# Last row tiles of a decoder step: stores from another queue, and sums ahead of the last turns

## The reference

```
x = x + (silu(ua_c) * ub) @ ffn_down              # 2816 -> 1024 features
y = x * rsqrt(mean(x * x, axis=-1) + 1e-6) * norm_final
y_prompt, y_sample = y[16:1040], y[1040:1072]     # stored as rows, one per token
```

## Time and profile before

| | |
|---|---|
| three runs | 1876.35, 1876.5, 1870.95 us; median 1876.35 |
| the profiled execution | 1874.11 us, of it 1872.3 us span |
| TensorE busy | 1722.2 us (92% of the span), mean granted clock 0.956 |
| VectorE, ScalarE, POOL busy | 1268.0 (68%), 682.0 (36%), 350.2 us (19%) |
| last `down` matmul ends | about 1849.0 us |

### The profile page before, as it was taken

The page is one execution under the profiler, slowest core; times in us unless marked ns, Lnnn a source line. Parts: engine busy times, 40 slices in busy tenths (PEclk is TensorE's granted clock), DMA queues, the critical chain, the costliest instruction groups (busy, mean ns, idle before and its releaser), DMA issues.

```text
span 1872.3 us, 30833 instructions
## 1 busy us (share of the span) xinstructions
PE 1722.2 (92%) x12025; PEld 1623.0 (87%) x12025; DVE 1268.0 (68%) x2319; ACT 682.0 (36%) x1207; POOL 350.2 (19%) x236
## 2 busy tenths in 40 slices
PE   4959999899999869988779989999999999999995
PEld 4834999899999857776679988999999999999995
DVE  4373766788888968867444378777777776575553
ACT  3253011121211146665542155333333334564442
POOL 0544143222222331132236220000000000000000
PEclk7979999999999979999889999999999999999997
DMA  7133211122222021343646212222222213866452
GB/s 261 46 92 93 57 46 40 54 67 92 85 80 63 15 102 64 119 146 132 208 129 245 93 47 80 81 82 80 70 81 87 75 58 117 292 200 210 153 181 77
DMA packets 161878, 201.28 MB, mean 108 GB/s; under 512 B 20057, under 2 KB 123449, under 8 KB 161201
## 3 DMA queue, kind: packets, MB, share of 16 engines
q1 hardware_dynamic: 142516, 124.66, 22.2%
q0 software_dynamic: 14256, 55.27, 8.9%
q10 hardware_dynamic: 4978, 19.59, 2.8%
HBM read 163.27 MB, written 35.61 MB: 106 GB/s over the span
## 4 chain that ended last, share of the span: by engine, by line
PE 53%; DVE 4%; ACT 3%; issue 2%; DMA 1%; POOL 0%; DVEq 0%; ACTq 0%
PE ps L2303 23%; PE ps L2696 13%; PE ps L229 6%; PE ps L1894 3%; PE ps L1938 2%; PE ps L1876 1%; PE ps L1860 1%; PE ps L1949 1%; PE ps L1975 1%; DMA down_raw<-in_ffn_down 1%; ACT probs L2082 0%; PE ps L2688 0%; DVE probs_turned L2160 0%; DVE operand_lo L3157 0%; DVE up_P_lo L3119 0%
## 5 line engine op out<-in xcount | busy, mean ns | idle before, releaser
L229 PE MATMUL ps<-act_hi,w_hi 128*128 128x358 f32 (+1 forms) x1080 | 360.8, 334 | 12.1 <-POOL act_lo L464 5.5
L2303 PE MATMUL ps<-operand_hi,up_P_hi 128*128 128x268 f32 x1232 | 354.3, 288 | 8.9 <-issue 6.7
L229 PE MATMUL ps<-act_lo,w_hi 128*128 128x358 f32 (+1 forms) x1080 | 354.9, 329 | 0.0
L229 PE MATMUL ps<-act_hi,w_lo 128*128 128x358 f32 (+1 forms) x1080 | 354.0, 328 | 0.0
L2303 PE MATMUL ps<-operand_lo,up_P_hi 128*128 128x268 f32 x1232 | 353.4, 287 | 0.0
L2303 PE MATMUL ps<-operand_hi,up_P_lo 128*128 128x268 f32 x1232 | 353.0, 287 | 0.0
L2303 PEld LDWEIGHTS ps<-operand_hi,up_P_hi 128*128 128x128 f32 x1232 | 233.9, 190 | 9.4 <-issue 7.0
L2303 PEld LDWEIGHTS ps<-operand_lo,up_P_hi 128*128 128x128 f32 x1232 | 233.4, 189 | 0.0
L2303 PEld LDWEIGHTS ps<-operand_hi,up_P_lo 128*128 128x128 f32 x1232 | 233.4, 189 | 0.0
L229 PEld LDWEIGHTS ps<-act_hi,w_hi 128*128 128x128 f32 (+1 forms) x1080 | 204.5, 189 | 14.5 <-issue 11.8
L229 PEld LDWEIGHTS ps<-act_lo,w_hi 128*128 128x128 f32 (+1 forms) x1080 | 205.0, 190 | 1.2
(11 more groups left out here) (423 smaller groups left out, 3128.0 us busy)
## 6 DMA issues: line engine op xcount, KB each, us to landing
down_raw<-in_ffn_down SPq DMA_DIRECT2D x132, 256.0 KB, 3.0
w_raw<-in_w_in SPq DMA_DIRECT2D x32, 512.0 KB, 3.9
w_raw<-in_ffn_up SPq DMA_DIRECT2D x48, 256.0 KB, 3.4
inner_save<-xt SPq DMA_DIRECT2D x22, 536.0 KB, 2.7
xt<-in_ffn_up SPq DMA_DIRECT2D x40, 256.0 KB, 3.4
inner_raw<-inner_save SPq DMA_DIRECT2D x44, 192.0 KB, 3.8
x_save<-xt SPq DMA_DIRECT2D x1, 4296.0 KB, 12.8
mix_b<-row ACTq DMA_DIRECT2D x8, 537.0 KB, 3.6
```

The costliest lines, as they stand in the source:

```text
L229: last = pe.matmul(core.acc(out_set)[0:rows, c, :], w(k), b(k)[:, c * CH:(c + 1) * CH], start=(i == 0 and n == 0), stop=(i == kblocks - 1 ...
L2303: last = pe.matmul(out[:, c, :], w[:, 128 * k:128 * k + 128], b(k)[:, cols], start=(name in OPENING and k == 0 and n == 0), stop=(k == 3 a ...
```

## The change

Five things, all in the stage above:

1. SP stores row tiles 6, 7 and 8 and the sample rows (new `store_row` in SP's block, semaphore `last_stored`), and waits for the four at its end. POOL stores row tiles 0 to 5 and waits for those.
2. In the last pass VectorE adds a square to the total after each eviction but the first (`between`); the last one follows.
3. TensorE turns features 0 to 6 of tiles 6 and 7, then of tile 8, then sums over features, and then turns feature 7 of the three tiles.
4. The copy of the sums out of PSUM is dropped: VectorE scales straight from PSUM, for the last third in two instructions.
5. The semaphore `y_taken` goes; in the first two thirds TensorE waits for the first count of `y_own` instead, before it turns the second row tile over the sums.

```diff
@@ block.sync
+        def store_row(t):
+            sp.wait_ge(out_a, t + 1)
+            sp.wait_ge(out_d, t + 1)
+            sp.dma_start(core.o["y_prompt"][0][128 * t - META:128 * t + QROWS[t] - META], rows[t % 3][0:QROWS[t], :])\
+                .then_inc(last_stored, 16)
+
+        for t in (6, 7, 8):
+            store_row(t)
+        sp.dma_start(core.o["y_sample"].rearrange("b s d -> (b s) d"), rows[(NT - 1) % 3][QROWS[-1]:ROWS[-1], :])\
+            .then_inc(last_stored, 16)
+        sp.wait_ge(last_stored, 64)
@@ block.tensor
+        def turn(t, k):
+            return pe.transpose(ysrc(t)[:, 128 * k:128 * k + 128], x[:, k, 128 * t:128 * t + ROWS[t]], core.c["ident"])
+
         def turn_rows(t):
-            n = ROWS[t]
             for k in range(KB):
-                if t == 6:
-                    pe.wait_ge(y_gain, 2 * KB + k + 1)
-                last = pe.transpose(ysrc(t)[:, 128 * k:128 * k + 128], x[:, k, 128 * t:128 * t + n], core.c["ident"])
+                last = turn(t, k)
             last.then_inc(turned, 1)
...
                 elif y == 1:
-                    pe.wait_ge(y_taken, third + 1)
+                    pe.wait_ge(y_own, ROOT_LINKS * third + 1)
...
-        turn_rows(6)
-        turn_rows(7)
+        for k in range(KB - 1):
+            pe.wait_ge(y_gain, 2 * KB + k + 1)
+            for t in (6, 7):
+                turn(t, k)
+        for k in range(KB - 1):
+            turn(8, k)
         sum_y(2)
-        turn_rows(8)
+        pe.wait_ge(y_gain, 3 * KB)
+        for t in (6, 7, 8):
+            turn(t, KB - 1).then_inc(turned, 1)
@@ block.gpsimd
-        for third in range(3):
-            if third < 2:
-                for s in (2 * third + 2, 2 * third + 3):
-                    pool.wait_ge(x_back[s % 2], 16 * (s // 2))
-                    x_reload(s)
+        for third in range(2):
+            for s in (2 * third + 2, 2 * third + 3):
+                pool.wait_ge(x_back[s % 2], 16 * (s // 2))
+                x_reload(s)
             for t in range(3 * third, 3 * third + 3):
                 store_row(t)
-        pool.dma_start(core.o["y_sample"].rearrange("b s d -> (b s) d"), rows[(NT - 1) % 3][QROWS[-1]:ROWS[-1], :])\
-            .then_inc(stored[(NT - 1) % 3], 16)
         for z in range(3):
-            pool.wait_ge(stored[z], 16 * (4 if z == 2 else 3))
+            pool.wait_ge(stored[z], 32)
         pool.wait_ge(states_stored, 32)
@@ block.vector
-        def evict(s):
+        def evict(s, between=None):
...
+                if between and m:
+                    between(m - 1)
...
             if third < 2:
-                dve.tensor_copy(ss, core.flat(7, 16)[:, cols]).then_inc(y_taken, 1)
+                dve.tensor_scalar(mean, core.flat(7, 16)[:, cols], 1.0 / D, EPS, ALU.mult, ALU.add).then_inc(y_own, 1)
             else:
-                dve.tensor_copy(core.ss[:, 6:8], core.flat(7, 16)[:, 6:8])
-                dve.tensor_copy(core.ss[0:ROWS[-1], 8:9], core.flat(7, 16, ROWS[-1])[:, 8:9]).then_inc(y_taken, 1)
-            dve.wait_ge(y_taken, third + 1)
-            dve.tensor_scalar(mean, ss, 1.0 / D, EPS, ALU.mult, ALU.add).then_inc(y_own, 1)
+                dve.tensor_scalar(core.mean[:, 6:8], core.flat(7, 16)[:, 6:8], 1.0 / D, EPS, ALU.mult, ALU.add)
+                dve.tensor_scalar(core.mean[0:ROWS[-1], 8:9], core.flat(7, 16, ROWS[-1])[:, 8:9], 1.0 / D, EPS,
+                                  ALU.mult, ALU.add).then_inc(y_own, 1)
...
-        evict(PASSES - 1)
-        for m in range(MG):
-            add_y(MG * (PASSES - 1) + m)
+        evict(PASSES - 1, lambda m: add_y(MG * (PASSES - 1) + m))
+        add_y(MG * PASSES - 1)
         y_roots(2)
```

More of the change, by code:

```diff
@@ L2412, in mix_and_ffn_stage @@
     y_sq, y_total, y_gain = sem("y_sq"), sem("y_total"), sem("y_gain")
-    y_summed, y_taken, y_rooted, y_own = sem("y_summed"), sem("y_taken"), sem("y_rooted"), sem("y_own")
+    y_summed, y_rooted, y_own = sem("y_summed"), sem("y_rooted"), sem("y_own")
     turned, out_a, out_d = sem("y_turned"), sem("y_out_a"), sem("y_out_d")
-    stored = [sem(f"y_stored{y}") for y in range(3)]
+    stored, last_stored = [sem(f"y_stored{y}") for y in range(3)], sem("y_last_stored")
     wo, wup, wdown = core.i["w_o"][0], core.i["ffn_up"][0], core.i["ffn_down"][0]
@@ L3401, in y_roots @@
             cols = slice(3 * third, 3 * third + 3)
-            ss, mean, root_, inv = (core.ss[:, cols], core.mean[:, cols], core.root[:, cols], core.inv[:, cols])
+            mean, root_, inv = core.mean[:, cols], core.root[:, cols], core.inv[:, cols]
             done = ROOT_LINKS * third
```

## The result

After: 1863.72 us, median of 17 runs (1859.58 to 1868.14); before, beside it: 1872.66, median of 17 (1868.82 to 1878.57). The ratio is 0.9943, with a 95% interval of 0.9934 to 0.9951: 9.2 to 12.4 us of 1872.66 are gone. The two medians alone lie 8.9 apart, a quotient of 0.9952; the ratio isn't their quotient, and by the times the gain is known to 2 or 3 us only. The forecast was 1864.0.

What follows compares the result with a forecast made beforehand. TensorE's matmuls bound the bulk (busy 92%); the change targets the 23.2 us tail. Terms -2.75 - 0.53 - 1.30 - 6.90 = -11.48 give 1864.9 us on the median, forecast 1864, range 1857 to 1869.5.

Steps and rivals of the forecast that it cites:

- Squares between evictions, sums ahead of the last turns: After the last down matmul: adds move into VectorE's gaps, sums start at 1851.18 against 1853.33, -2.15 us.
- Copy dropped from the roots: Between sums and row scaling: VectorE scales straight from PSUM, net -0.15 us.
- The clock: TensorE's sums: without idling before them the clock stays at 1.00, 0.90 us instead of 1.35, -0.45.
- SP issues: From first finished row half to its store: SP issues 0.03 us behind it instead of POOL's 0.56, -0.53.
- Transfers: First issue to last landing of the four last stores: 4.53 us instead of 5.83, -1.30.
- the smaller estimate: Last stores' transfers: by the Trainium skill the queue change gives some 0.4 us, making the forecast sum 0.9 smaller.
- bound of -1.48: Largest gain allowed for the last stores' transfers, in us, if SP's issues close up.
- The end: Last landing to span end: POOL's DRAIN runs earlier beside down matmuls, 2.03 us instead of 8.93, -6.90.
- the DRAIN stays at the end: Rival, block end: the 6.84 us belong to closing the block, gain only -4.6, about 1872 us; 5%.
- SP would pay instead: Rival, block end: a DRAIN costs 0.082 us per DMA of its engine, SP's takes 24.7, 1890 us; 3%.
- the chain gets shorter but the store doesn't: Rival, tail: transfers gain nothing, TensorE falls to half clock before the sums, -9.7, 1866.6 us; 20%.
- it shows: Opposite of a rival on the whole time: run spread of 5.55 us hides the gain, within 0.3%; 5%.

Runs made afterwards that it cites:

- stores-alone kernel: Kernel before the change, with only SP issuing row tiles 6 to 8 and the sample rows; 1866.59 against 1874.62 us, ratio 0.9956.

## Why the prediction was right, step by step

- **Squares between evictions, sums ahead of the last turns.** Row scaling starts 2.9 sooner after M; -2.75 was forecast. The sums start 2.14 after M, 2.15 forecast, and take 0.82 where 0.90 was taken from the earlier trace rows. Undoing one reorder costs +1.0, the other +1.1, as the two runs show. One reading was loose: of ScalarE's 1.49 ahead of its last square the adds held only 0.44; the other 1.05 is still there in the changed kernel. The sum used the 0.44.
- **Copy dropped from the roots.** -0.20 against -0.15: from VectorE's first use of the sums to the rows 1.55 before, 1.35 after. No run tries it by itself.
- **The clock.** The term of -0.45 came out (1.35 to 0.82), but its reason isn't shown. The forecast tied the lower level to TensorE's idle time before the sums; with an idle of 1.69 in the old order the level stayed at 1.00 until after the sums, and with 2.13, in the kernel before and in the stores-alone kernel, it was at 0.50 and 0.51 when they ran (stores alone: the row below). What decides between these stays open, so the term came out in part by luck.

```profile
1854.80:1857.00 2.20, 2.20 (x14) 2.18 (x12) 0.14 (x1) 0.00 (x0) 0.00 (x0) 0.51 0.00 0
```

- **SP issues.** -0.48 against -0.53: the 0.08 that SP took, instead of 0.03.
- **Transfers: the mis-sized term.** -0.7 against -1.30. The step took the landing of a 536 KB store with nothing behind it, 2.7, for the last one here. But the last one is a 128 KB store from 32 partitions, and it took 3.4; the closer issues (1.70 from the first to the last, against 1.83) gave 0.13 back. Spread over the partitions as many rows land in 2.7. That this is just the forecast's number is partly chance: the term left out that the DMA engines have 1.25 MB to move, which at 401 GB/s is 3.1 of the 5.10 (an estimate from the window above), so that a store issued last waits for those ahead of it. The same store took 4.0 from POOL, so the change of queue gave 0.6, less than the 1.1 that the term took from 3.8 and 2.7; the smaller estimate that the prediction set beside the term was nearer. The term's bound of -1.48 has no row behind it. The row of the `y_sample` store itself, 4.0 for 128 KB beside 3.8 for 512 KB, had shown that the small one isn't the quicker.
- **The end.** -7.07 against -6.90: the DRAIN went under the `down` matmuls, and SP's DRAIN took 0.007 instead of the 0.124 that was put down for it. SP started it 0.19 after the last landing; the 0.15 put down for that had no row behind it.
- Sum: -2.9 - 0.48 - 0.7 - 7.07 = -11.15, against -11.48 forecast and -11.1 in the spans.
- **The time itself.** That 1863.72 lies 0.3 from the forecast is luck: the forecast started from 1876.35, the median of three runs, and the median of 17 is 1872.66. From there the sum gives 1861.2. The terms are what was right, not the last digits of the time.

**The rivals.** That the DRAIN stays at the end fell with 1.86 between last landing and end. The Trainium skill (VectorE: DVE Perf Modes, The DRAIN you can't avoid) has drains around a kernel at a constant of about 12 ns on all engines; SP's 7 ns is near that, POOL's 6513 to 8310 ns, by its count of DMAs, aren't. That SP would pay instead fell with SP's 7 ns: the price per DMA is POOL's. Its arithmetic, 0.082 a DMA, was right for POOL. That the chain gets shorter but the store doesn't was half right: of the 1.3 that the transfers were to give only 0.7 came, but the sums ran at full clock. The gain is twice what this measurement can tell from no change, so it shows.

## What to carry to other kernels

Look at the end of the program behind the last landing: a DRAIN of POOL's there can be a price per DMA that POOL issued, and here it ran under TensorE's work for nothing once POOL's list ended early. So let another queue make the last stores, and don't let POOL wait for them. In a tail of several engines, a reorder removes one wait and the next one then counts, so value it by what comes last after it; here either wait, left in place, cost 1 us, though removing one alone gave less than half of that at the same clock. And size a last store by one of its own shape: here a store of few rows from neighbouring partitions wasn't quicker than a large one.

## What the runs showed of the hardware that was not expected

- POOL's closing DRAIN grew with its DMAs in the block, about 82 ns each (79, 83 and 101 of them), and didn't shrink though the transfers had landed 50 us before; at two earlier block ends, with 16 each, it ended 1.4 us behind POOL's last work. SP's, with more DMAs in the last block, is 7 ns.
- DMA engines that the profile shows as fully busy (1.03 to 1.07) moved 401, 131 or 126 GB/s, the low figures where 16 or 32 neighbouring partitions are read.
- SP's issue of the sample rows took 1.14 us, ScalarE's of the same store 0.39.
- An idle gap of TensorE of 1.69 or 1.25 ahead of the sums left the granted clock at 1.00.
